# Two transfers change places in SyncE's queue before layer 2's experts

## The chip, the cores and the metric

The kernel runs on one core of one Trainium2 chip. The metric is the device time of one execution in microseconds. Every transfer spoken of here is issued by SyncE (SP) or, for gathers and scatters, by GpSimd (POOL), and all of them run on the core's 16 DMA engines.

## The reference

Two residual layers over 512 tokens of width 1024. Each ends in a hierarchical mixture of experts:

```
def hierarchical_moe(xn, w_rg, b_rg, w_re, b_re, w_gate, w_up, w_down):
    lg = (jnp.einsum('bsd,dg->bsg', xn, w_rg) + b_rg).astype(jnp.float32)
...
    for g in range(N_EXPERT_GROUPS):
        h = jax.nn.silu(jnp.einsum('bsd,edf->bsef', xn, w_gate[g])) * jnp.einsum('bsd,edf->bsef', xn, w_up[g])
        y = y + jnp.einsum('bsef,efd->bsd', h * combine[:, :, g, :, None], w_down[g])
    return y
```

Each token goes to one of 4 groups and to 2 of the 8 experts in it. Each of the 32 experts has a gate and an up matrix of 1024x256 and a down matrix of 256x1024, in float32: 3 MB an expert and layer. Ahead of the experts layer 1 has a mixer with attention and layer 2 a pooling mixer, and both normalise the rows first.

## The kernel before

The 32 experts of a layer are worked off as 16 pairs. A pair takes 64 token slots for each of its two experts. For each pair, POOL gathers the rows of its tokens from `norm_rows` in DRAM, TensorE (PE) transposes them (line 2196), multiplies by gate and up (line 2202, 32 matmuls), transposes the hidden values (line 2209) and multiplies by down (line 2220, 16 matmuls), and POOL scatters the result to `expert_rows`. The rows of pair 0 are picked by matmuls; the first gather is that of pair 1, and in layer 2 it waits for the first table of the router (line 852) and for all four stores of normalised rows (line 853).

The weights stream from DRAM all the time. Gate and up of a pair are 4 MB and down is 2 MB. There are three buffers for gate and up; pair 2 of layer 2 has the one that is called `norm`, whose first half (NORM[:, 0:4096]) holds the normalised rows `xs` until they are stored, and whose second half is free when all four blocks of the pooling mixer have been added (`s_x3` at 4). SP issues every weight load in an order written out by hand, and waits between them on semaphores that PE and others raise. A transfer is only handed to the DMA engines when SP comes to it.

At the start of layer 2's experts SP's order is (lines 618 to 653): the stores of the normalised rows of blocks 0, 1 and 2, each behind its rows; after the mixer's last add, three transfers that bring pair 3's down (`load_down_extra`, 1 MB, 0.5 MB and 0.5 MB); the store of block 3; `load_down_early(1, 1)`, 0.5 MB of pair 4's down; `load_gate_up(1, 2, 1)`, the 2 MB of pair 2's second expert; then a wait until all four stores have landed, since what comes next overwrites them (`load_gate_up(1, 2, 0)`, 2 MB of pair 2's first expert); `load_down_early(1, 0)`, 1 MB; and then quarters of 1 MB for pairs 3 and 4, each behind a quarter of the gate and up of pairs 0 and 1 on PE. In the arguments layer 2 is `l == 1`.

Of the kernel before, what the change touches and what calls it, by code (L numbers as in the profile page):

```python
# [45 lines left out]
def build(nc, t):  # L46
    ctx = ExitStack()
    with ctx:
# [431 lines left out]
        def _(sp):  # L480
# [12 lines left out]
            def load_gate_up_part(l, i, a, c):  # L493

                s = SLOTS[l][i % 3]
                e = l * NE + 2 * i + a
                sp.dma_start(gu[s][:, a, c], wgu[e, :, c]).then_inc(s_gul[a][s], 16)

            def load_gate_up_steps(l, i, j, n):

                s = SLOTS[l][i % 3]
                e = l * NE + 2 * i
                c = slice(4096 // n * j, 4096 // n * (j + 1))
                sp.dma_start(gu[s][:, :, c], wgu[e:e + 2, :, c].rearrange("a p n -> p a n"))\
                  .then_inc(s_gul[2 * j // n][s], 16)
# [8 lines left out]
            def load_gate_up(l, i, h):  # L514

                if i in HALVED:
                    load_gate_up_steps(l, i, h, 2)
                else:
                    load_gate_up_part(l, i, h, slice(0, 4096))
# [9 lines left out]
            def load_down_early(l, a):  # L529
                e = l * NE + 8 + a  # L530
                c = slice(0, D if a else 2 * D)
                sp.dma_start(dn_early[:, 2 * D * a:2 * D * a + c.stop], wd_rows[e:e + 1, :, c]
                             .rearrange("a p f -> p (a f)")).then_inc(s_dnx, 16)
# [66 lines left out]
            for l in range(LAYERS):  # L600
                n = 1 + 2 * l
                def store_rows(b):

                    sp.wait_ge(s_xs[b], n)
                    sp.dma_start(norm_dram[b * P:(b + 1) * P, :], (xs if l else xs0)[:, b, :]).then_inc(s_st, 16)

                def load_down_extra(a, c):

                    e = l * NE + 6 + a
                    sp.dma_start(dn_extra[:, a, c], wd_rows[e:e + 1, :, c].rearrange("a p f -> p (a f)"))\  # L610
                      .then_inc(s_dnx, 16)
# [13 lines left out]
                if l == 0:  # L625
                    load_gate_up_part(0, 1, 1, slice(2 * D, 4 * D))
                    load_down_extra(0, whole)
                    sp.wait_ge(s_st, 16 * (NB - 1))
                    load_down_extra(1, front)
                    sp.wait_ge(s_op, 2 * NB + 1)  # L630
                    load_gate_up_part(0, 2, 1, slice(3 * D, 4 * D))
                    store_rows(NB - 1)
                    sp.wait_ge(s_lg, NB)
                    load_down_early(0, 0)
                    sp.wait_ge(s_st, 16 * NB)
                    load_down_extra(1, back)
                else:
                    sp.wait_ge(s_x3, NB)
                    load_down_extra(0, whole)
                    load_down_extra(1, front)  # L640
                    load_down_extra(1, back)
                    store_rows(NB - 1)
                    load_down_early(1, 1)
                    load_gate_up(1, 2, 1)
                    sp.wait_ge(s_st, 16 * NB * 2)
                    load_gate_up(1, 2, 0)
                    sp.wait_ge(s_lg, NB * 2)
                    load_down_early(1, 0)
# [1872 lines left out]
```

## Time and profile before

| | |
|---|---|
| median of 3 runs | 809.83 us (809.79 to 810.35) |
| the profiled execution | 810.39 us, its span 808.6 us |
| mean granted TensorE clock | 0.983 |
| PE busy | 760.3 us, 94% of the span |
| moved by DMA | 258.69 MB, mean 320 GB/s |

The profile is of one execution. The span runs from the first to the last instruction, and 1.8 us of the time lie around it. Times in the views are us from the start of the span.

### The profile page before, as it was taken

The numbers are of one execution on the slowest core, as the hardware profiler recorded it, in microseconds if no ns is written. First come the engines' busy times: TensorE is split into PE (matmuls) and PEld (weight loads), VectorE is DVE, ScalarE is ACT, GpSimd is POOL, SyncE is SP. The second block draws the span as 40 slices with busy tenths as digits, with TensorE's granted clock in tenths as the row PEclk, the third lists the DMA queues.
The fourth block names the chain that finished last, engine by engine and source line by source line (L and its number), as shares of the span: only waits on it lengthen the run. The fifth ranks groups of instructions, "written<-read, shape, count | busy, mean of one in ns | idle before, by whom it ended". The sixth has DMA issues, their size and how long they took to land.

```text
span 808.6 us, 9731 instructions
## 1 busy us (share of the span) xinstructions
PE 760.3 (94%) x3822; PEld 356.3 (44%) x3824; DVE 259.3 (32%) x654; ACT 251.2 (31%) x599; POOL 104.0 (13%) x170
## 2 busy tenths in 40 slices
PE   8999999999999999999988989979999999977987
PEld 7544544555555654333333333369333333332322
DVE  1011517675646365111110011376631111111015
ACT  4421346464444632121121112256222112111112
POOL 3000000000000001212422112250111121101111
PEclk9999999999999999999998989999999999999999
DMA  8995225132010679999999999999999999999998
GB/s 336 347 342 226 94 77 209 53 131 105 1 40 1 214 295 344 423 423 426 420 426 427 425 421 420 401 431 408 401 409 426 424 424 424 427 425 426 422 403 322
DMA packets 39703, 258.69 MB, mean 320 GB/s; under 512 B 8145, under 2 KB 8529, under 8 KB 26600
## 3 DMA queue, kind: packets, MB, share of 16 engines
q1 hardware_dynamic: 31016, 242.22, 74.0%
q0 software_dynamic: 8640, 15.83, 5.2%
q8 instruction: 31, 0.51, 0.2%
q14 instruction: 16, 0.13, 0.0%
HBM read 247.46 MB, written 26.21 MB: 338 GB/s over the span
## 4 chain that ended last, share of the span: by engine, by line
PE 85%; DMA 5%; DVE 4%; issue 4%; ACT 2%; SPq 0%; POOL 0%; POOLq 0%; DVEq 0%
PE ps L2202 28%; PE ps L2220 13%; PE ps L1893 12%; PE ps L2044 7%; PE ps L2196 4%; PE ps L1960 3%; PE ps L2102 3%; PE ps L1972 2%; PE ps L2111 2%; DMA norm<-expert_rows 2%; DMA expert_rows<-tmp 2%; PE ps L2149 2%; PE ps L1875 2%; PE ps L2209 1%; DVE x_rows L1308 1%
## 5 line engine op out<-in xcount | busy, mean ns | idle before, releaser
L2202 PE MATMUL ps<-w_pair,tmp 128*64 128x512 f32 x704 | 165.1, 620 | 17.3 <-issue 14.6
L2202 PEld LDWEIGHTS ps<-w_pair,tmp 128*64 128x64 f32 x704 | 52.8, 142 | 112.0 <-issue 105.9
L1893 PE MATMUL ps<-w_pair,norm 128*128 128x512 f32 (+1 forms) x256 | 98.6, 545 | 1.2 <-DMA w_pair<-in_w_in_chunk_dram 1.2
L1282 DVE TENSOR_TENSOR tmp<-tmp,ps 128x256 f32<-128x256 f32 x32 | 13.5, 421 | 249.0 <-ACT tmp L1141 249.0
L1141 ACT ACTIVATE tmp<-ps 128x256 f32<-128x256 f32 x32 | 12.3, 384 | 231.1 <-PE ps L2202 231.1
L2202 PE MATMUL ps<-norm,tmp 128*64 128x512 f32 x320 | 74.0, 617 | 6.0 <-issue 6.0
L2220 PE MATMUL ps<-w_pair,tmp 128*64 128x512 f32 x296 | 70.1, 599 | 1.1 <-ACT tmp L1144 0.9
L1893 PEld LDWEIGHTS ps<-w_pair,norm 128*128 128x128 f32 x256 | 48.2, 190 | 48.7 <-issue 44.4
L828 POOL DMA_INDIRECT expert_rows<-tmp x30 | 30.2, 1005 | 304.5 <-DVE tmp L1740 278.4
L822 POOL DMA_INDIRECT tmp<-norm_rows,tmp x30 | 31.1, 1035 | 262.1 <-DVE tmp L1660 237.7
L1740 DVE COPY tmp<-ps 128x512 f32<-128x512 f32 x30 | 20.8, 692 | 89.1 <-PE ps L2220 89.1
L2202 PEld LDWEIGHTS ps<-norm,tmp 128*64 128x64 f32 x320 | 23.6, 142 | 48.9 <-issue 48.0
L2220 PE MATMUL ps<-rest,tmp 128*64 128x512 f32 x192 | 43.8, 598 | 1.1 <-ACT tmp L1144 1.1
L1136 ACT ACTIVATE tmp<-ps,small_vectors 128x128 f32<-128x128 f32 x120 | 34.3, 368 | 24.4 <-PE ps L2196 24.4
L1150 ACT ACTIVATE tmp<-ps 128x512 f32<-128x512 f32 x30 | 17.9, 597 | 76.1 <-PE ps L2220 76.1
L1105 ACT ACTIVATE rest<-ps 128x768 f32<-128x768 f32 (+3 forms) x32 | 21.6, 676 | 59.6 <-PE ps L2102 59.6
L2196 PEld LDWEIGHTS ps<-ident,tmp 128*128 128x128 f32 x240 | 29.0, 194 | 24.3 <-issue 21.1
L2220 PEld LDWEIGHTS ps<-w_pair,tmp 128*64 128x64 f32 x296 | 20.1, 136 | 34.6 <-issue 29.9
L2196 PE MATMUL ps<-ident,tmp 128*128 128x128 f32 x240 | 34.7, 288 | 0.0
L1072 ACT ACTIVATE extra<-ps,mix_small 128x384 f32<-128x384 f32 (+3 forms) x64 | 32.3, 511 | 3.4 <-DVE mix_small L1496 3.1
L1960 PE MATMUL ps<-w_pair,norm 128*128 128x512 f32 x64 | 29.5, 596 | 1.8 <-ACT tmp L1044 1.1
L1282 DVE TENSOR_TENSOR ps<-ps,masks 128x256 f32<-128x256 f32 x40 | 16.5, 430 | 42.0 <-PE ps L1972 41.8
(288 smaller groups left out, 879.2 us busy)
## 6 DMA issues: line engine op xcount, KB each, us to landing
w_pair<-in_gate_up_by_row_dram SPq DMA_DIRECT2D x30, 2048.0 KB, 27.6
norm<-in_gate_up_by_row_dram SPq DMA_DIRECT2D x18, 2048.0 KB, 20.5
w_pair<-in_down_by_pair_dram SPq DMA_DIRECT2D x15, 2048.0 KB, 33.0
w_pair<-in_gate_up_by_row_dram SPq DMA_DIRECT2D x28, 1024.0 KB, 10.8
rest<-in_down_by_pair_dram SPq DMA_DIRECT2D x10, 2048.0 KB, 27.9
w_pair<-in_w_in_chunk_dram SPq DMA_DIRECT2D x4, 2048.0 KB, 14.6
norm<-expert_rows SPq DMA_DIRECT2D x16, 512.0 KB, 7.1
expert_rows<-tmp SPq DMA_DIRECT2D x1, 4096.0 KB, 41.6
```

The lines of the kernel that those rows point to most:

```text
L822: return pool.indirect_dma_start(out=buf, out_offset=None, in_=norm_dram, in_offset=bass.IndirectOffsetOnAxis(ap=index, axis=0), bounds_ch ...
L828: return pool.indirect_dma_start(out=out_dram, out_offset=bass.IndirectOffsetOnAxis(ap=index, axis=0), in_=buf, in_offset=None, bounds_che ...
L1072: ins = a.activation(prob[:, n % 2, h, 0:width], bank(2 * (n % 2) + h)[:, 0:width], ACT.Exp, bias=nmax[:, 2 * n + h:2 * n + h + 1], accum_ ...
L1136: ins = a.activation(xT[:, k, :], bank(0)[:, k * P:(k + 1) * P], ACT.Copy, scale=gain_v[:, n, k:k + 1])
L1282: return ve.tensor_tensor(out, in0, in1, op)
L1893: ins = mm(bank(4 + i % 4)[:, 0:n], xT[:, b, k, :], w[:, k, :], start=(k == 0), stop=(k == KD - 1))
L1960: ins = mm(bank(7), xT[:, b, k, :], w[:, k, :], start=(k == 0), stop=(k == KD - 1))
L2044: ins = mm(out_bank(b, half), xT[:, b, k, :], wout[half][:, k, :], start=(j == first), stop=(j == last - 1))
L2102: ins = te.transpose(bank(4 + a // 2)[:, (a % 2) * 256 + h * P:(a % 2) * 256 + (h + 1) * P], prob[:, n % 2, h, a * P:(a + 1) * P], ident[: ...
L2196: ins = te.transpose(bank(k // 4)[:, (k % 4) * P:(k % 4 + 1) * P], xv[:, k, :], ident[:, :])
L2202: ins = mm(o[64 * a:64 * a + 64, :], xT[:, k, 64 * a:64 * a + 64], gu[w][:, a, 2 * FE * k:2 * FE * (k + 1)], start=(k == 0), stop=(k == KD ...
L2220: ins = mm(bank(4 + half)[64 * a:64 * a + 64, :], hT[:, jj, 64 * a:64 * a + 64], d, start=(jj == 0), stop=(jj == 1))
```

## The change

The issue of the 2 MB of pair 2's second expert is moved up by two places: it now stands ahead of the store of the last block of normalised rows and of the 0.5 MB of pair 4's down. No transfer, wait or instruction is added or taken away.

```
                     load_down_extra(1, back)
+                    load_gate_up(1, 2, 1)
                     store_rows(NB - 1)
                     load_down_early(1, 1)
-                    load_gate_up(1, 2, 1)
                     sp.wait_ge(s_st, 16 * NB * 2)
                     load_gate_up(1, 2, 0)
```

## Rows read from the trace of the kernel before

**Rows 1.** The page: busy tenths and GB/s in 40 slices of 20.2 us.

```profile
PE   8999999999999999999988989979999999977987
GB/s 336 347 342 226 94 77 209 53 131 105 1 40 1 214 295 344 423 423 426 420 426 427 425 421 420 401 431 408 401 409 426 424 424 424 427 425 426 422 403 322
```

**Rows 2.** Chain that ended last, pairs 10 to 13 of layer 2: start, us, what.

```profile
698.27 1.41 issue
...
711.89 4.09 issue
...
729.62 2.74 issue
...
746.25 2.39 issue
```

**Rows 3.** Windows: length, busy us of PE, PEld, DVE, ACT, POOL, granted clock, DMA share, GB/s.

```profile
564.00:568.00 4.00, 3.94 (x24) 2.18 (x25) 3.11 (x23) 1.07 (x2) 0.00 (x0) 0.67 0.95 262
568.00:600.00 32.00, 30.43 (x156) 12.81 (x155) 18.18 (x80) 8.40 (x24) 3.05 (x3) 0.99 1.02 414
600.00:690.00 90.00, 90.00 (x436) 33.92 (x433) 13.33 (x22) 18.27 (x52) 16.22 (x16) 1.00 1.02 424
690.00:760.00 70.00, 59.37 (x264) 23.59 (x262) 8.34 (x14) 11.13 (x33) 8.11 (x8) 0.93 1.01 424
```

**Rows 4.** Timeline of SP's queue, 559 to 596 us: start, us, what it issues.

```profile
559.30 3.26 SPq L610 DMA_DIRECT2D rest<-in_w_exp_down_dram  x3
563.59 0.33 SPq L605 DMA_DIRECT2D norm_rows<-norm  x1
563.96 0.64 SPq L532 DMA_DIRECT2D extra<-in_w_exp_down_dram  x1
564.64 8.14 SPq L497 DMA_DIRECT2D norm<-in_gate_up_by_row_dram  x2
572.83 0.43 SPq L532 DMA_DIRECT2D extra<-in_w_exp_down_dram  x1
579.76 16.41 SPq L504 DMA_DIRECT2D w_pair<-in_gate_up_by_row_dram  x8
```

**Rows 5.** Waits of SP's queue, 556 to 582 us.

```profile
SPq L497 <- DMA norm_rows<-norm: 7.3, 1, 7.3
```

**Rows 6.** By line: the last store, and the 2 MB behind it, issue to landing.

```profile
L605 SPq DMA_DIRECT2D norm_rows<-norm x1: 327/327/327, 563.6 to 563.6; - x1
...
DMA to landing us min/median/max: 8.8/8.8/8.8
...
L497 SPq DMA_DIRECT2D norm<-in_gate_up_by_row_dram x1: 502/502/502, 564.6 to 564.6; - x1
...
DMA to landing us min/median/max: 13.9/13.9/13.9
```

**Rows 7.** Layer 1's transfers on idle DMA engines: SP's timeline, windows, issues.

```profile
294.16 0.33 SPq L605 DMA_DIRECT2D norm_rows<-rest  x1
...
297.07 0.33 SPq L610 DMA_DIRECT2D rest<-in_w_exp_down_dram  x1
...
294.50:295.00 0.50, 0.50 (x4) 0.37 (x4) 0.20 (x1) 0.50 (x1) 0.00 (x0) 1.00 0.08 33
...
norm_rows<-rest SPq DMA_DIRECT2D x1, 512.0 KB, 2.9
...
w_pair<-in_gate_up_by_row_dram SPq DMA_DIRECT2D x1, 1024.0 KB, 6.4
```

**Rows 8.** Timeline of all engines: the first gather of layer 2 and its user.

```profile
576.70 0.16 DVE L1660 TENSOR_SCALAR tmp<-ps 128x1 int32<-128x1 f32 x1 [1.59 <-PE ps L2161]
...
577.66 1.06 POOL L822 DMA_INDIRECT tmp<-norm_rows,tmp  x1 [30.93 <-DVE tmp L1660]
...
582.69 3.65 PE L2202 MATMUL ps<-w_pair,tmp 128*64 128x512 f32 x16
...
586.28 0.97 PEld L2196 LDWEIGHTS ps<-ident,tmp 128*128 128x128 f32 x8 [0.81 <-DMA tmp<-norm_rows,tmp]
```

More of the change, by code:

```diff
@@ L641, in _ @@
                     load_down_extra(1, back)
+                    load_gate_up(1, 2, 1)
                     store_rows(NB - 1)
                     load_down_early(1, 1)
-                    load_gate_up(1, 2, 1)
                     sp.wait_ge(s_st, 16 * NB * 2)
```

## The prediction

> **What bounds the kernel now.** I read the page's slices first. From the 17th slice on (323 us) PE is nearly full and the DMA engines move 401 to 431 GB/s in every slice but the last two [rows 1]. Two resources seem full at once, so I asked the windows which of them sets the end. From 600 to 690 us PE never rests (90.00 of 90.00 us), and DMA is full too. From 690 to 760 us PE is busy for 59.37 of 70 us, while DMA goes on at the same 424 GB/s [rows 3]. The chain that ended last has its gaps just there: 1.41, 4.09, 2.74 and 2.39 us ahead of the gate and up of four pairs running, 10.6 us together [rows 2]. They are called "issue", but PE's next matmul needs the weights that are still on their way. So in layer 2 PE lives at first on buffers filled ahead, uses up that lead by 698 us, and is paced by the stream of weights from then on. Hence the rule by which I cost everything: a microsecond in which the DMA engines move nothing between 560 and 700 us comes out at the end in full, and a microsecond that PE loses before 690 us costs nothing, since it only makes one of those gaps shorter (cover 10.6 us).
>
> One place stands out in the stream: 564 to 568 us, 262 GB/s where the neighbours have 414 to 424 [rows 3]. Against 425 GB/s that is 4 x (425 - 262) = 652 KB, or 1.5 us of the stream. It is the largest thing that this edit could win.
>
> **The change, part by part.** It adds and removes nothing: the same transfers, issued in another order. So there are three questions: when does each land, does the stream get a new hole, and does the old hole go.
>
> *Order of landing.* The store is issued at 563.59 and lands 8.8 us later, at 572.4; the 2 MB of gate and up, issued at 564.64, lands 13.9 us later, at 578.5 [rows 4, 6]. Between the two landings lie 6.1 us, and the bytes issued between, 0.5 + 2 MB (2.62 million bytes), take 6.2 us at 425 GB/s. The queue is served in the order of issue, so I can compute the new landings. At 425 GB/s 0.5 MB takes 1.23 us and 2 MB takes 4.93 us. Gate and up goes ahead of the store and lands at 572.4 - 1.23 + 4.93 = 576.1. The store lands at 577.3, 4.9 us later than before, and the early down at 578.5, where the three ended before.
>
> *SP and its wait.* SP now issues gate and up at about 562.6, when the three extra downs are out (559.30 + 3.26) [rows 4], in the 1.0 us in which it waits for the last rows; then the store at 563.6 and the early down, at most 0.5 us late. Behind them stands the wait for the stores, which took 7.3 us [rows 5] and now lasts from 564.6 to 577.3. Queued behind it are the 2 MB of pair 2's first expert, the 1 MB of early down, and then the quarters. The first quarter is issued at 579.76 [rows 4], when PE lets go of it, and SP is through with the two others by 578.3, so the quarters are not late. Pair 2's weights are needed by PE two pairs of about 12 us after 577 us; 2 us of lateness don't show.
>
> *The new hole.* Before, 2.5 MB stood behind the store, 6.2 us of work, and SP issued more as soon as the store had landed; the stream never noticed. Now 0.5 MB stands behind it, 1.23 us. What has to be bridged is the way from the store's last byte to the first byte of the next transfer. Layer 1 shows it on idle engines: a store of 0.5 MB issued at 294.16 lands 2.9 us later, and SP's next issue follows at 297.07; in the half microsecond up to 295.0 only 33 GB/s move, that is, the first bytes come some 0.8 us after the issue [rows 7]. Of the 2.9 us 0.8 are that start and 1.23 the bytes, so 0.87 pass between the last byte and the landing. The bridge is 0.87 + 0.05 for SP + 0.8 = 1.7 us, less 1.23 covered: a hole of **0.5 us**, the lower bound. Upper bound, also from layer 1: 1 MB of gate and up on engines that had stood idle took 6.4 us [rows 7], of which 2.47 are bytes and 0.87 the landing, so 3.06 us start. That gives 0.87 + 0.05 + 3.06 - 1.23 = **2.75 us**; but a gather ran beside it. The coming transfer has the long rows of the usual stream and the engines have only just run out, so I am nearer to the first row: I take **0.8 us**.
>
> *The first gather.* POOL issues it at 577.66, 0.8 us after the router's first table is there (576.70 + 0.16) [rows 8]. Now the store lands at 577.3, 0.4 us after the table, so the gather goes out at 578.1. PE works on pair 0's gate and up until 586.34 and its weight load for the transposes had waited 0.81 us for the gather [rows 8], so the gather was barely in time, and 0.4 us later means up to 0.4 us lost by PE. It is off the bound, by the cover named above: price nothing, 0.4 us if that cover were gone.
>
> *The old hole.* Would 2 MB more in the queue fill it? The transfers in service between 564 and 568 us had been issued by 562.6 [rows 4], and the store landed only at 572.4: bytes already in the queue were enough for the whole hole, yet they went slowly. In a queue served in order, something put behind them can't help. Against that, SP's pause from 562.56 to 563.59 ends just ahead of the hole. I take 0, with a bound of -1.5 us.
>
> Sum: +0.8 (hole) + 0 (gather) + 0 (old hole) = +0.8 us on the profiled execution's 810.39, so 811.2. That execution was 0.56 us above the median of the runs, 809.83; on the median it gives **810.6 us**, 0.1% more. A measurement of this kernel can tell about 0.2%, 1.6 us, from no change, so this is "same".
>
> **The rivals.**
> 1. *The old hole is filled.* If the slow stretch came from SP's pause, the 2 MB issued into it wins up to 1.5 us: 809.83 - 1.5 + 0.8 = 809.1 with the new hole, 808.3 if the gather's bytes or the engines' unequal ends hide that one too. For it speaks only the place of the pause. Chance 0.22, of which 0.09 is faster by over 0.2%.
> 2. *The store's landing is slow, and the new hole is long.* This is the one on the other side. The price is what the bridge exceeds 1.23 us by, and it decides from a bridge of 2.9 us on: between 1.6 and 2.75 us of hole, 811.5 to 812.6. For it: the stream is full where layer 1's was empty, and the 6.4 us row. Against it: the 2.9 us row, a store of just this shape. Chance 0.18. In the Trainium skill, "DMA: Bandwidth & Descriptors", section "Latency and other measured facts", HBM access takes 0.2 us on average and 2 us at high load, and most of a transfer's fixed cost is the receipt of its last write. By that page the 0.87 us could be 2 us here, an estimate of 2 + 0.85 - 1.23 = 1.6 us of hole and 811.4 us; no row of this case shows a store's receipt in a full stream by itself.
> 3. *Nothing happens.* The 16 engines end their shares at different moments, the hole is spread and partly filled by gathers, and the later stream absorbs what is left: 809.8, within 0.3 us. Chance 0.15.
>
> **How the numbers follow.** The forecast (810.3 to 811.3) has 0.45, the rivals 0.22, 0.18 and 0.15. Faster by over 0.2% is only the filled hole without a new one, 0.09, and a little for what I haven't seen: 0.10. Slower by over 0.2% is rival 2 and a little of the forecast's upper edge: 0.19. Same is the rest, 0.71. The range leaves out 0.08 below and some 0.1 above: 808.7 to 811.9.
>
> **What the profile after would show.** SP's queue: gate and up issued at 562.6, the store at 563.6 to 564.1, SP's wait for the stores some 12 to 13 us instead of 7.3, the next issue of line 497 at about 577.3. The store's time to landing: 13 to 14 us instead of 8.8. Windows of 1 us: one near 577 to 579 us well below 425 GB/s, and 564 to 568 us still at about 262. POOL's first gather at about 578.1. The gaps ahead of pairs 10 to 13 together 0.5 to 1 us longer. The prediction is wrong if the store overtakes the 2 MB (the queue isn't served in order, then there is no new hole), if 564 to 568 us comes out at 400 GB/s, or if the gaps don't change although the stream has lost time.

## The result: 0.2% slower

| | before | after |
|---|---|---|
| median of 10 runs each | 809.89 us | 811.73 us |
| lowest to highest | 809.1 to 811.63 | 810.29 to 812.64 |
| profiled execution (its span) | 810.39 us (808.6) | 810.81 us (809.1) |
| mean granted clock | 0.983 | 0.985 |

The ratio of the two is put at 1.0020, with a 95% interval of 1.0012 to 1.0028: 1.6 us slower, between 1.0 and 2.3. (The two medians by themselves are 1.8 us apart; everything below goes by the ratios.) One single execution, of the run a1_cover below, took 4311 us and is in no ratio. On the 809.83 us that the forecast started from, that is 811.5 us. It lies in the range (808.7 to 811.9), but twice as far from "no change" as the 0.8 us forecast, and right at the 0.2% at which the prediction drew the line between "same" and "slower". So the question for the runs is where the other 0.8 us comes from.

The page of the kernel after, its slices of 20.2 us (GB/s, as in [rows 1]):

```profile
GB/s 347 330 313 262 92 86 200 53 143 93 1 40 1 223 285 344 424 424 424 422 426 425 424 421 421 413 430 410 360 408 425 426 420 427 426 425 426 423 414 334
```

The 29th slice, 566 to 586 us, has 360 GB/s where before had 401: there the change acts. What happened in it stands in SP's queue, kernel after (start, us, what it issues), to be held against [rows 4]:

```profile
561.89 0.82 SPq L497 DMA_DIRECT2D norm<-in_gate_up_by_row_dram  x1
562.98 0.33 SPq L605 DMA_DIRECT2D norm_rows<-norm  x1
563.35 0.61 SPq L532 DMA_DIRECT2D extra<-in_w_exp_down_dram  x1
576.37 0.33 SPq L497 DMA_DIRECT2D norm<-in_gate_up_by_row_dram  x1
576.75 0.43 SPq L532 DMA_DIRECT2D extra<-in_w_exp_down_dram  x1
578.50 17.56 SPq L504 DMA_DIRECT2D w_pair<-in_gate_up_by_row_dram  x8
```

SP's waits in the kernel after, 556 to 584 us (before: [rows 5]):

```profile
SPq L497 <- DMA norm_rows<-norm: 12.4, 1, 12.4
```

And the same issues by line, kernel after, each with its time from issue to landing (before: [rows 6]); the last two are what SP issues once the wait is over:

```profile
L497 SPq DMA_DIRECT2D norm<-in_gate_up_by_row_dram x1: 818/818/818, 561.9 to 561.9; - x1
...
DMA to landing us min/median/max: 13.2/13.2/13.2
...
L605 SPq DMA_DIRECT2D norm_rows<-norm x1: 326/326/326, 563.0 to 563.0; - x1
...
DMA to landing us min/median/max: 13.4/13.4/13.4
...
L532 SPq DMA_DIRECT2D extra<-in_w_exp_down_dram x1: 611/611/611, 563.3 to 563.3; - x1
...
DMA to landing us min/median/max: 14.2/14.2/14.2
...
L497 SPq DMA_DIRECT2D norm<-in_gate_up_by_row_dram x1: 328/328/328, 576.4 to 576.4; - x1
...
DMA to landing us min/median/max: 8.1/8.1/8.1
...
L532 SPq DMA_DIRECT2D extra<-in_w_exp_down_dram x1: 432/432/432, 576.7 to 576.7; - x1
...
DMA to landing us min/median/max: 10.3/10.3/10.3
```

The 2 MB lands at 575.1, the store at 576.4, the early down at 577.6, in the order of issue and 1.2 us apart. The store takes 13.4 us instead of 8.8, SP waits 12.4 us instead of 7.3, and when it goes on, the 1.2 us of early down are all that is left to move. The windows of the kernel after show the stream there (columns as in [rows 3]):

```profile
564.00:568.00 4.00, 3.42 (x21) 1.66 (x22) 3.42 (x21) 0.46 (x2) 0.00 (x0) 1.00 1.01 378
...
600.00:690.00 90.00, 90.00 (x434) 34.03 (x434) 13.32 (x22) 18.27 (x52) 16.24 (x16) 1.00 1.02 424
690.00:760.00 70.00, 59.20 (x264) 23.37 (x262) 8.33 (x14) 11.13 (x33) 8.11 (x8) 0.93 1.01 424
...
574.00:575.00 1.00, 0.52 (x4) 0.52 (x5) 0.00 (x0) 0.42 (x1) 0.00 (x0) 1.00 0.84 344
575.00:576.00 1.00, 1.00 (x13) 0.69 (x12) 0.53 (x3) 0.74 (x3) 0.00 (x0) 1.00 0.58 238
576.00:577.00 1.00, 1.00 (x4) 0.20 (x4) 0.90 (x4) 0.78 (x3) 0.00 (x0) 1.00 0.25 102
577.00:578.00 1.00, 1.00 (x8) 0.29 (x4) 0.90 (x6) 0.98 (x3) 0.79 (x1) 1.00 1.16 250
578.00:579.00 1.00, 1.00 (x8) 0.56 (x4) 0.93 (x4) 0.84 (x2) 0.27 (x1) 1.00 0.59 197
579.00:580.00 1.00, 1.00 (x8) 0.36 (x8) 1.00 (x3) 0.82 (x4) 0.00 (x0) 1.00 0.93 377
```

The six rows from 574 to 580 us sum up to 1508 (344 + 238 + 102 + 250 + 197 + 377), where 6 x 425 = 2550 would be full; (2550 - 1508) / 425 = 2.45 us of the stream are missing. The hole begins at about 575 us, *before* the store has landed at 576.4 and while 0.5 MB is still to come, and the stream is not full again before 579 us. Neither was in the forecast. At 564 to 568 us, where before had 262 GB/s, there are 378. PE is full from 600 to 690 us and paced by the stream behind it, as before.

The gaps in the chain that ended last, kernel after, pairs 10 to 13 (before: [rows 2]):

```profile
698.16 1.67 issue
...
712.03 4.12 issue
...
729.90 2.64 issue
...
746.43 2.37 issue
```

Together 10.80 us, 10.63 before: 0.2 us more, where the runs say 1.6. Part of this is where the one execution stood. SP's queue starts the first store of layer 2 at 548.15 in the profile of before and at 547.55 here:

```profile
547.55 8.95 SPq L605 DMA_DIRECT2D norm_rows<-norm  x3
```

The kernel after was 0.6 us ahead when it came to the change, and the spans differ by 0.5 us for all that. So from here on times are counted from the first of these stores. Counted so, pair 13's gap ends at 748.80 - 547.55 = 201.25 after and at 746.25 + 2.39 - 548.15 = 200.49 before, 0.8 us later.

A better measure than the gaps is the landing of the last of these transfers (the early down of 1 MB that is issued at 576.75). It lands 576.75 + 10.3 - 547.55 = 39.5 us after the first store. Before, by line:

```profile
L532 SPq DMA_DIRECT2D extra<-in_w_exp_down_dram x1: 431/431/431, 572.8 to 572.8; - x1
...
DMA to landing us min/median/max: 13.6/13.6/13.6
```

That is 572.83 + 13.6 - 548.15 = 38.3 us. The *hole* I measure between two landings: from that of the last transfer issued ahead of SP's wait to that of the last one of the group, less their bytes at 425 GB/s. After: 587.05 - 577.55 = 9.50 for 3 MB, which take 7.40: 2.1 us. Before: 586.43 - 578.54 = 7.89, less 7.40: 0.5 us.

### The profile page after: what moved, and what is told of

Read it like the earlier page. It is cut to its first block, busy times and chain, and to the rows that moved or that the text cites. A ratio compares the mean times of both kernels' runs of the same rounds, so it can differ in the third digit from the quotient of the medians.

```text
span 809.1 us, 9731 instructions
## 1 busy us (share of the span) xinstructions
PE 759.7 (94%) x3822; PEld 357.6 (44%) x3824; DVE 259.2 (32%) x654; ACT 251.4 (31%) x599; POOL 104.0 (13%) x170
## 4 chain that ended last, share of the span: by engine, by line
PE 80%; DMA 10%; DVE 4%; issue 3%; ACT 2%; SPq 1%; POOLq 0%; DVEq 0%
PE ps L2202 25%; PE ps L2220 12%; PE ps L1893 12%; PE ps L2044 7%; DMA w_pair<-in_gate_up_by_row_dram 4%; PE ps L2196 4%; PE ps L1960 3%; PE ps L2102 3%; PE ps L1972 2%; PE ps L2111 2%; DMA norm_rows<-norm 2%; DMA norm<-expert_rows 1%; PE ps L2209 1%; PE ps L1875 1%; DMA tmp<-norm_rows,tmp 1%
## 5 line engine op out<-in xcount | busy, mean ns | idle before, releaser
L2220 PEld LDWEIGHTS ps<-w_pair,tmp 128*64 128x64 f32 x296 | 20.1, 136 | 34.3 <-issue 29.9
L1960 PE MATMUL ps<-w_pair,norm 128*128 128x512 f32 x64 | 29.5, 596 | 1.8 <-ACT tmp L1044 1.1
## 6 DMA issues: line engine op xcount, KB each, us to landing
w_pair<-in_gate_up_by_row_dram SPq DMA_DIRECT2D x30, 2048.0 KB, 29.9
w_pair<-in_gate_up_by_row_dram SPq DMA_DIRECT2D x28, 1024.0 KB, 13.6
```

The costliest lines, as they stand in the source:

```text
L1960: ins = mm(bank(7), xT[:, b, k, :], w[:, k, :], start=(k == 0), stop=(k == KD - 1))
L2220: ins = mm(bank(4 + half)[64 * a:64 * a + 64, :], hT[:, jj, 64 * a:64 * a + 64], d, start=(jj == 0), stop=(jj == 1))
```

## The experiments

Every kernel was timed in five rounds beside the kernel before, a1 to a4, b1 to b4 and c1 each as a group; the kernel before had medians of 810.12, 809.69 and 809.30 us in the three groups, so between groups only the ratios can be compared. I name the transfers by SP's code: H is the 2 MB of pair 2's second expert (`load_gate_up(1, 2, 1)`), S the last store, D the early down of 0.5 MB, W the wait for the stores, L the 2 MB behind it (`load_gate_up(1, 2, 0)`), E the early down of 1 MB behind the wait for the gathers. Before: S D H W L E. After: H S D W L E.

**a1_cover: H first, but 1.5 MB behind the store.** H S D E W L.

```
                     load_down_early(1, 1)
-                    sp.wait_ge(s_st, 16 * NB * 2)
-                    load_gate_up(1, 2, 0)
                     sp.wait_ge(s_lg, NB * 2)
                     load_down_early(1, 0)
+                    sp.wait_ge(s_st, 16 * NB * 2)
+                    load_gate_up(1, 2, 0)
```

> The changed kernel, with the 1 MB of early down (load_down_early(1, 0), behind its own wait for the logits) issued before SP's wait for the stores, so that 1.5 MB instead of 0.5 MB stand behind the last store (3.7 us of cover for a bridge of about 2.9 us). The store stays behind the 2 MB and the first gather stays late. Theory H (the price is the hole in the stream of weights while SP waits for the store): the low windows at 575 to 579 us go, and the time falls back to that of the kernel before or a little under it, 808.7 to 810.1 us. Theory G (the price is the first gather, which waits for the late store and makes PE wait some 1 us): as slow as the changed kernel, 811.0 to 812.0 us, with the hole gone from the windows.

Measured: median 810.21 us, ratio 1.0004 (0.9994 to 1.0014), 0.1 us above the expected range and level with the kernel before beside it. The store still takes 13.1 us and SP still waits 11.1 us for it, but the window shows a full stream in the place of the hole (kernel a1_cover):

```profile
574.00:580.00 6.00, 6.00 (x35) 2.68 (x35) 4.72 (x16) 4.47 (x12) 1.06 (x1) 1.00 1.00 408
```

A late store and a long wait cost nothing as long as SP has left enough behind the store. H ahead of the store costs nothing by itself.

**a2_nocover: nothing behind the store.** H D S W L E.

```
                     load_gate_up(1, 2, 1)
-                    store_rows(NB - 1)
                     load_down_early(1, 1)
+                    store_rows(NB - 1)
                     sp.wait_ge(s_st, 16 * NB * 2)
```

> The changed kernel, with the 0.5 MB of early down also issued ahead of the last store, so that nothing stands behind the store. Theory H: the hole grows by the 1.23 us that the 0.5 MB covered, and the store lands 1.2 us later still; 1.0 to 1.3 us above the changed kernel, 812.6 to 813.2 us. Theory G: the gather goes out 1.2 us later still, PE waits about 2.3 us for it instead of 1.1, and the time also grows by about 1.2 us, so this run alone doesn't tell the two apart: a1_cover and a4_late_gather do. A third theory, that the difference of before and after is only scatter between builds: 810 to 811.7 us.

Measured: median 811.76 us, ratio 1.0023 (1.0014 to 1.0033), 1.9 us. The expectation was missed: 812.6 to 813.2 us had been put down. The hole did grow by 1.2 us against the kernel after (see the table), but the time by only 0.3, which is within the noise of the two. The wait and the stream, kernel a2_nocover:

```profile
SPq L497 <- DMA norm_rows<-norm: 13.7, 1, 13.7
```
```profile
574.00:575.00 1.00, 0.55 (x2) 0.00 (x0) 0.61 (x3) 0.41 (x1) 0.00 (x0) 1.00 0.74 303
575.00:576.00 1.00, 0.76 (x11) 0.75 (x12) 0.00 (x0) 0.19 (x1) 0.00 (x0) 1.00 0.66 270
576.00:577.00 1.00, 1.00 (x10) 0.47 (x6) 0.73 (x4) 0.97 (x4) 0.00 (x0) 1.00 0.32 131
577.00:578.00 1.00, 1.00 (x5) 0.34 (x6) 0.93 (x3) 0.78 (x3) 0.00 (x0) 1.00 0.03 12
578.00:579.00 1.00, 1.00 (x6) 0.14 (x2) 0.86 (x8) 0.98 (x2) 0.33 (x1) 1.00 0.94 197
579.00:580.00 1.00, 1.00 (x8) 0.73 (x8) 0.97 (x4) 0.66 (x3) 0.73 (x1) 1.00 0.66 147
580.00:581.00 1.00, 1.00 (x6) 0.32 (x6) 1.00 (x2) 1.00 (x4) 0.00 (x0) 1.00 0.78 311
581.00:582.00 1.00, 1.00 (x16) 0.30 (x13) 0.14 (x1) 0.08 (x1) 0.00 (x0) 1.00 0.93 393
```

This is the hole with nothing to cover it. SP issues the next 2 MB at 577.84. The stream has been thinning out since 574, nearly 4 us ahead of the store's landing, and needs until 581 to be full again, 3 us after the issue. Two ramps, where the forecast had one flat stretch of 0.87 + 0.8 us. The trace's packet records (start and duration of each packet) say more of both. The last 4 KB packet of the store ends at 577.46, so its landing comes 0.4 us after its last byte. The first packet of the next 2 MB starts at 578.78, 0.9 us after the issue, and the first 15 of its 16 KB packets take 0.7 to 1.9 us each, where such a packet takes 0.61 us in the full stream (median).

**a3_before_early_first: the control of a1.** The order of before with E ahead of the wait, as in a1: S D H E W L. The edit is that of a1, made on the kernel before.

> The kernel before, with only the 1 MB of early down moved ahead of SP's wait for the stores. The store stands where it stood before, and the cover behind it grows from 2.5 to 3.5 MB, which was not needed. Theory H: as the kernel before, 809.3 to 810.5 us. Theory G: the same. It is the control for a1_cover: if this too is faster than before, a1_cover's time has to be compared with this one.

Measured: median 810.44 us, ratio 1.0002 (0.9993 to 1.0011). So E's place has no price that can be seen, and a1 against a3 is the swap alone, with the stream covered in both: 810.21 against 810.44. In this pair 564 to 568 us moved 389 GB/s with H first and 294 with S first, and the time did not follow.

**a4_late_gather: only the gather late.** The kernel before, but POOL holds layer 2's first gather until H has landed:

```
                 pool.wait_ge(s_st, 16 * NB * (l + 1))
+                if l:
+                    pool.wait_ge(s_gul[1][2], gate_up_count(1, 2))
                 gather_rows(xg[1], second_now).then_inc(s_xg[1], 16)
```

> The kernel before, with POOL's first gather of layer 2 also waiting for the 2 MB of pair 2's second expert to land (about 578.5 us), so that it goes out about 1 us later, as in the changed kernel, while the stream of weights has no hole. Theory H: PE waits about 1 us for the gather, and the gaps ahead of pairs 10 to 13 take it back; as the kernel before, 809.3 to 810.6 us. Theory G: about 1 us slower, 810.8 to 811.6 us.

Measured: median 809.96 us, ratio 0.9999 (0.9990 to 1.0008). Timeline of POOL and PE, kernel a4_late_gather (in brackets the idle time ahead and what ended it):

```profile
578.48 1.20 POOL L822 DMA_INDIRECT tmp<-norm_rows,tmp  x1 [32.78 <-DMA norm<-in_gate_up_by_row_dram]
...
585.87 1.16 PE L2198 MATMUL ps<-ident,tmp 128*128 128x128 f32 x8 [1.20 <-DMA tmp<-norm_rows,tmp]
```

The kernel after has the gather at 577.21 (POOL's timeline), and PE waits 1.08 us for it:

```profile
586.17 1.16 PE L2196 MATMUL ps<-ident,tmp 128*128 128x128 f32 x8 [1.08 <-DMA tmp<-norm_rows,tmp]
```

Here PE waits just as long (1.20 us), and the kernel is not slower. The gather is not the cause of the 1.6 us: the interval of a4 ends at 0.6.

**b1_before_again and b2_after_again.** Both kernels unchanged, for a second profile of each.

> The kernel before, unchanged, as a second profile of it and as a measure of how much two builds of one program scatter. In the first profile of it the windows at 564 to 568 us showed 262 GB/s, in the profiles of four other orders 294, 347, 343 and 389. Theory H (the hole behind the late store is the price): ratio 1.000, 809.4 to 810.6 us, the stretch 575 to 582 us full, and the old hole somewhere between 260 and 350 GB/s by chance. The theory that scatter of builds makes the difference: a ratio outside 0.999 to 1.001.

> The changed kernel, unchanged. Theory H: ratio 1.001 to 1.003 again, and the stream loses again some 2.3 us in the seven microseconds in which SP waits for the store and starts anew. Scatter of builds: a ratio nearer to 1.000.

Measured: 810.3 us, 1.0005 (0.9996 to 1.0013), and 810.95 us, 1.0020 (1.0011 to 1.0028). The ratio of the change repeats to the digit. In b2 SP waits 12.8 us, the hole is 2.05 us and the last landing comes at 40.2; in b1 they are 0.5 and 37.7. The low stretch at 564 to 568 us is 301 GB/s in b1 and 412 in b2. Over all profiles, those of the runs below too, it is 262, 301, 294, 347 and 286 with the store first (before, b1, a3, a4, b3) and 378, 412, 389, 343 and 335 with H first (after, b2, a1, a2, b4), on the mean some 0.7 us of stream better with H first; c1, whose store another engine issues, has 308. The two groups overlap, and the granted clock differed too: it was 0.50 to 0.71 in these 4 us in before, b1, a3, b3 and b4 and 1.00 in the others. Nor are the three transfers together clearly through any sooner: the last of them lands 30.4, 29.8, 29.9 and 30.5 us after the first store of layer 2 in before, b1, a3 and a4, and 30.0, 30.7, 29.4, 29.5 and 28.5 us in after, b2, a1, a2 and b4.

**b3_store_first_short_cover: the hole without the swap.** The store goes out first, as before, but H stands behind the wait: S D W H L E. The kernel after, with

```
                     load_down_extra(1, back)
-                    load_gate_up(1, 2, 1)
                     store_rows(NB - 1)
                     load_down_early(1, 1)
                     sp.wait_ge(s_st, 16 * NB * 2)
+                    load_gate_up(1, 2, 1)
                     load_gate_up(1, 2, 0)
```

> The last store stands where it stood before, but pair 2's second expert is issued behind SP's wait for the stores, so that only the 0.5 MB of early down stands behind the store, as in the changed kernel. The store lands early (about 572 us) and the first gather is on time. Theory H: the hole is as long as in the changed kernel, about 2.3 us, at 571 to 575 us instead of 576 to 579, and the time is that of the changed kernel, 811.2 to 812.2 us. Theory G (the late store and gather are the price): as the kernel before, 809.5 to 810.5 us.

Measured: median 811.49 us, ratio 1.0019 (1.0011 to 1.0028), 1.5 us. The store lands 8.9 us after its issue, POOL's gather goes out as soon as its table is there, and PE waits 0.15 us for it; none of what the swap delays is late. Yet the time is that of the change, and the hole is there, 4 us earlier (windows, kernel b3_store_first_short_cover):

```profile
571.00:572.00 1.00, 1.00 (x11) 0.61 (x10) 0.25 (x2) 0.00 (x0) 0.00 (x0) 1.00 0.43 176
572.00:573.00 1.00, 1.00 (x3) 0.47 (x3) 0.93 (x5) 0.00 (x0) 0.00 (x0) 1.00 0.07 29
573.00:574.00 1.00, 1.00 (x3) 0.38 (x2) 0.93 (x6) 0.00 (x0) 0.00 (x0) 1.00 1.34 262
```

**b4_cover_1mb: 1 MB behind the store.** The kernel after, with E cut into two halves, one of them ahead of the wait: H S D E' W L E''. PE's wait for these downs counts the one transfer more.

```
                     load_down_early(1, 1)
+                    sp.wait_ge(s_lg, NB * 2)
+                    e, cc = NE + 8, slice(0, D)
+                    sp.dma_start(dn_early[:, cc], wd_rows[e:e + 1, :, cc].rearrange("a p f -> p (a f)")).then_inc(s_dnx, 16)
                     sp.wait_ge(s_st, 16 * NB * 2)
                     load_gate_up(1, 2, 0)
-                    sp.wait_ge(s_lg, NB * 2)
-                    load_down_early(1, 0)
+                    e, cc = NE + 8, slice(D, 2 * D)
+                    sp.dma_start(dn_early[:, cc], wd_rows[e:e + 1, :, cc].rearrange("a p f -> p (a f)")).then_inc(s_dnx, 16)
...
-                        pe_.wait_ge(s_dnx, 80 * (l + 1))
+                        pe_.wait_ge(s_dnx, 80 * (l + 1) + 16 * l)
```

> The changed kernel with one half (0.5 MB) of the 1 MB early down ahead of SP's wait for the stores: 1 MB stands behind the last store. With 0, 0.5 and 1.5 MB behind it the stream lost 3.5, 2.3 and 0.3 us there. Theory H: about 1.1 us lost, that is 1.2 us less than in the changed kernel, and the time half way, 810.3 to 811.2 us. If the loss is a fixed price of waiting whatever stands behind the store: 2.3 us and 811.7 us.

Measured: median 810.34 us, ratio 1.0006 (0.9997 to 1.0015), 0.5 us; the time is in the expected range, the hole of 1.5 us is longer than the 1.1 expected. The window, kernel b4_cover_1mb:

```profile
574.00:580.00 6.00, 5.31 (x28) 2.13 (x27) 4.00 (x22) 3.72 (x8) 1.06 (x1) 1.00 0.93 330
```

330 GB/s lies between the 213 of b2 and the 408 of a1 in the same window.

**c1_store_by_act: the store from another queue.** After b4 one thing was open: is the store late because SP's queue is served in order, or because the engines are full? Here it goes out from ACT's queue, right after ACT has scaled the last rows; SP's order is H D W L E.

```
                     load_gate_up(1, 2, 1)
-                    store_rows(NB - 1)
                     load_down_early(1, 1)
...
             rows(3, 3)
+            act.wait_ge(s_xs[3], 3)
+            act.dma_start(norm_dram[3 * P:4 * P, :], xs[:, 3, :]).then_inc(s_st, 16)
```

> Changed order, but the store of the last normalised rows goes out from ACT's queue right after the rows are scaled, and no longer from SP's queue behind the 2 MB of gate and up. SP's order is the 2 MB, the last early down, the wait, pair 2's second 2 MB, the gathers' wait, the first early down: nothing but 1 MB of early downs stands in front of the wait together with the 2 MB, and nothing behind the store on SP's queue. Theory 1 (the stream runs dry because the store lands last, whoever issues it; the engines serve the queues together, packet by packet): the store lands 3 to 6 us after its issue, SP's wait shrinks to 2 to 5 us while some 2 MB are still outstanding, there is no hole at 575 to 578, the gather is on time, and the time is that of before, 809.3 to 810.6. Theory 2 (the engines serve what they were given first, whatever the queue): the store takes 12 to 14 us again, SP waits as long as in the changed kernel, nothing stands behind the store, and the time is 811.3 to 812.0 with a hole.

Measured: median 809.93 us, ratio 1.0007 (0.9998 to 1.0016), 0.6 us. ACT's issue and SP's wait, kernel c1_store_by_act, by line and by waits:

```profile
L1267 ACTq DMA_DIRECT2D norm_rows<-norm x1: 373/373/373, 562.1 to 562.1; - x1
...
DMA to landing us min/median/max: 10.8/10.8/10.8
```
```profile
SPq L497 <- DMA norm_rows<-norm: 10.3, 1, 10.3
```
```profile
574.00:580.00 6.00, 6.00 (x34) 2.34 (x33) 4.61 (x16) 4.48 (x12) 1.06 (x1) 1.00 1.00 416
```

Half a hit. The store overtakes H: issued 0.9 us behind it, it lands at 572.9, while H lands at 561.2 + 14.7 = 575.9 and D at 577.1. So the order holds within a queue and not between two, and 4.2 us of stream are left when SP goes on: no hole. But the store took 10.8 us and not 3 to 6. By the packet records its first packet starts at 566.35, 4.2 us after the issue, when the last 8 KB packets of pair 3's down, which SP had issued ahead of H, are starting (566.58), and its packets run on among those of H until 572.35. A queue of its own is no fast lane here; that the engines were full with what SP had issued before fits these times, and no run tests it by itself. My other theory, no overtaking and a hole, is refuted.

**All runs together.** "Left" is what SP has issued behind the store when it lands; landings are counted from the first store of layer 2. In a1 the landing of L is not in the trace.

| kernel | order | left, MB | hole, us | last landing, us | time against before |
|---|---|---|---|---|---|
| before | S D H W L E | 2.5 | 0.5 | 38.3 | |
| b1 | the same | 2.5 | 0.5 | 37.7 | +0.4 (-0.3 to 1.1) |
| a4 | the same, gather late | 2.5 | 0.55 | 38.4 | -0.1 (-0.8 to 0.6) |
| a3 | S D H E W L | 3.5 | 0.4 | 37.7 | +0.2 (-0.6 to 0.9) |
| c1 | H D W L E, S by ACT | about 1.8 | 0.55 | 38.4 | +0.6 (-0.2 to 1.3) |
| a1 | H S D E W L | 1.5 | not read | not read | +0.3 (-0.5 to 1.1) |
| b4 | H S D E' W L E'' | 1.0 | 1.5 | 38.6 | +0.5 (-0.2 to 1.2) |
| after | H S D W L E | 0.5 | 2.1 | 39.5 | +1.6 (1.0 to 2.3) |
| b2 | the same | 0.5 | 2.05 | 40.2 | +1.6 (0.9 to 2.3) |
| b3 | S D W H L E | 0.5 | 1.9 | 39.9 | +1.5 (0.9 to 2.3) |
| a2 | H D S W L E | 0 | 3.3 | 40.2 | +1.9 (1.1 to 2.7) |

Of what was varied, the time goes with what is left behind the store alone: neither with H's place (a1, c1 against after; b3 against before) nor with the gather's. It does not go with it step by step: from 0.5 to 0 MB the hole grows by 1.2 us and the time by 0.3, and at 1 MB the hole is 1.0 us over that of before and the time 0.5, an interval that reaches below 0.

## Why the prediction came near, and what it had wrong

**The bound held; the rule made from it held for the landings, and only in part for the hole.** The last landing comes 1.5 to 2.2 us later in after, b2, b3 and a2 than the 38.0 that the first four rows of the table have on the mean, and their times are 1.5 to 1.9 us longer. A delay of the stream at 575 us comes out at the end, about in full, through 120 us in which PE hides it. A hole comes out in full in after, b2 and b3 (1.4 to 1.6 us over that of before, 1.5 to 1.6 us of time), but not in a2 (2.8 us over it, 1.9 us of time). That PE's own losses there cost nothing that can be seen is shown by a4.

**The order of landing, and SP's wait: held.** Forecast were landings at 576.1, 577.3 and 578.5; read are 575.1, 576.4 and 577.6, in an execution 0.6 us ahead. SP's wait is 12.4 us (12 to 13), the store's landing 13.4 us (13 to 14).

**The gather and the quarters: held, with one size wrong.** The gather is issued at 577.21; forecast was 578.1, which less the 0.6 us is 577.5. PE waits 1.08 us for it (1.89 in b2), where the forecast had up to 0.4; by a4 the price of that is nothing all the same. SP is through with the two others at 577.2, and the quarters start at 578.50.

**The new hole: the place was right, the size was half of what it is.** This is the step that failed. The prediction put it at 0.8 us: a bridge of 0.87 + 0.05 + 0.8 us, less 1.23 us of cover, is 0.5 us, and the row that gave 2.75 us as an upper bound moved it up by only 0.3. Read are 2.1 us, 1.6 over the 0.5 that before has without a wait of this kind. The mis-sized term is the start. The 2 MB issued into the queue that had just run dry land after 8.1 us; with 4.93 of bytes and 0.87 of landing that leaves **2.3 us for the start, not 0.8** (2.2 in b2, 2.1 in a2). Then 0.87 + 2.3 - 1.23 = 1.9 us, the hole. I had argued that I was nearer to the row of the small store on idle engines, since the engines "have only just run out"; it was the other row, 1 MB of gate and up with 3.06 us, that the start comes near to. A first byte after 0.8 us (0.9 us in a2) says nothing of when all engines are full again: in a2 the first packets of the 2 MB took 0.7 to 1.9 us instead of 0.61. The landing term was not too small but too large: 0.4 us in a2 and, by the packet records of the kernel before, 0.4 us in layer 1 too, where the store's last packet ends at 296.63 and the landing is at 297.06; the rest of the 0.87 us was bytes that took 1.65 us and not 1.23. With 0.4 us for the landing the start is 2.8 us and the sum the same, since the two are read together from the 8.1 us.

There is a second half to it that the formula does not have: the cover leaks. With 0, 0.5 and 1 MB behind the store the hole is 3.3, 2.1 and 1.5 us. The first 0.5 MB took off 1.2 us, what its bytes take; the second one 0.6. The windows of a2 show why it can: the stream thins out from 574 on, so some engines are through with their share some 3 us before the last one, and on those the cover is used up while the store is still on its way. One more sign of it is how far apart the engines are when they come to E. The trace's packet records have the first and the last start of its 128 packets of 8 KB (us):

```
before 4.81   b1 5.51   a3 5.08   a4 5.72   a1 5.14   c1 5.10
after  3.08   b2 2.90   b3 2.60   a2 2.86
```

At 425 GB/s these packets take 2.47 us. Where the stream never ran dry they start over 4.8 to 5.7 us, with the engines up to 3 us apart; behind a hole they start over 2.6 to 3.1 us. That the hole evens the engines out, and that this is why 2.45 us of missing bytes cost only 1.6 us of time, fits these numbers, but no run was made for it alone: it is argued, not shown.

**The old hole: price 0, held in the time; its reason was not.** Forecast was that 564 to 568 us stays at about 262 GB/s. It came out at 378, and over all profiles H first is better by some 0.7 us of bytes on the mean, with the two groups overlapping. But its landings are not clearly earlier, and a1 and a3, which differ in this alone, are 0.2 us apart. So "wrong if 564 to 568 us comes out at 400 GB/s" has nearly come to pass, and the gain of rival 1 has not. One part of the reason stands: the engines were busy for 0.95 of these 4 us while they moved 262 GB/s [rows 3], so the stretch is one of slow packets and not of missing work. Why they are slow, and why they are less so in the window with H first, stays open.

**The rivals.** Rival 1 (filled hole, 809.1 or 808.3) fell with a1. Rival 3 (nothing) fell with the result and with b2 and b3. Rival 2 (long hole, from 811.5 on) has the time that came, at its lower edge, 811.5, but it called the store's landing slow, and that is not what made the hole long. The estimate from the Trainium skill, "DMA: Bandwidth & Descriptors", section "Latency and other measured facts", 1.6 us of hole and 811.4 us, meets the number. But it put 2 us into the receipt of the store's last write in a full stream. The packet records of a2 have 0.4 us from the end of the store's last packet to its landing, as on idle engines in layer 1; so as far as packet records show a receipt, the 2 us aren't there, and the agreement is luck. The windows of a2 put the loss on both sides of the landing: 303, 270 and 131 GB/s ahead of it are engines that are through early, and 197, 147 and 311 behind it are the restart.

**The sign in the gaps.** Forecast were 0.5 to 1 us more in the gaps of pairs 10 to 13; read are 0.2. That sign was too weak to ask for: the executions of one kernel lie 2 to 3 us apart, and only counted from a common point (0.8 us at pair 13) does it show.

None of the kernels tried beats the one before.

## What to carry to other kernels

In a kernel paced by its stream, look at each wait of the queue that feeds it, and count the bytes issued behind the transfer that it waits for: here 0.5 MB cost 1.6 us, 1 MB some 0.5 us (not clear of nothing), and with 1.5 MB no price was left. How long the wait is does not matter (11.1 us in a1 were free), nor does its place; a wait near the end of what has been issued costs the running-out and the refilling, with nothing behind it a hole of 3.3 us and 1.9 us of time. Price the restart from a row with the size of the transfer that restarts, not from the smallest one.

## What the runs showed of the hardware

- A stream of 425 GB/s does not stop and start at once. With nothing left in the queue (a2) it thinned out over nearly 4 us before the last landing (303, 270, 131, 12 GB/s) and took 3 us after the next issue to be full (197, 147, 311, 393). 2 MB issued then took 7.9 to 8.1 us to land (a2, b2, after), of which 4.93 us are bytes at 425 GB/s; the first packet started 0.9 to 1.0 us after the issue, and the first 15 packets of 16 KB took 0.6 to 1.9 us each, where the median in the full stream is 0.61.
- A 0.5 MB store landed 0.4 us after the end of its last packet, in a stream that was running out (a2) as on idle engines (layer 1, before).
- Two queues were served side by side (c1): a store from ACT's queue landed 3.0 us ahead of 2 MB that SP had issued 0.9 us before it, but after 10.8 us, with the engines full. Within SP's queue the landings that were read kept the order of issue, to 0.1 us.
